# A two-layer transformer block with expert choice and a second mixer block: a reshaped router product, fewer count products, and modulation, squares and weight splits at other places

## Chip, cores and metric

One core of a Trainium2 chip runs the whole program; there is no traffic with other cores. The metric is the device time of one execution in microseconds (us), the median of three runs. The profile is of one execution; its times are microseconds from the start of its span.

## What is computed

512 latent tokens and 256 context tokens of width 1024 go through two layers and then one further block. Cut to what matters:

```python
for l in (0, 1):
    mod  = silu(c)     @ w_ada[l] + b_ada[l]       # 1024 -> 6144: six shifts, scales, gates
    modc = silu(c_ctx) @ w_ada[l] + b_ada[l]       # the same for the context
    h = modulate(rmsnorm(x), sh1, sc1);  p = h @ w_in[l]
    x = x + gt1 * mixer(p)        # two attentions, a short convolution,
                                  # three gated branches, @ w_out
    h2 = modulate(rmsnorm(x), sh2, sc2)
    x = x + gt2 * experts(h2)
# the context takes the same steps in layer 0 only

def experts(h):                                    # 16 experts, hidden 1024
    aff = softmax(h @ w_router, axis=experts)      # w_router: 1024 x 16
    gate, idx = top_k(aff, cap)                    # per expert 64 tokens (context 32)
    y = (silu(h[idx] @ w_g) * (h[idx] @ w_u)) @ w_d
    return scatter_add(y * gate)
```

Layer 1 works on the 512 latent tokens alone. The further block (`x2`) has a norm, a dilated and a latent attention, gated branches, an output product and a two-matrix feed-forward. Everything is float32; large products are made of three rounded-float32 ones.

## The kernel before

**Layout.** Activations stand transposed in on-chip memory: `XT[128, 8, 768]` has channel 128k+p in row k of partition p and the tokens along the columns (512 latent, 256 context). The program is written once for each engine, as functions in stage order (`pe_program`, `act_program`, `dve_program`, `pool_program`, `sp_program`, L2403 to L2497): start, then for each layer projection, attention, merge, choice and experts, then the second block. Nothing reorders the work; each engine takes its instructions in the written order, and counted semaphores tie the engines together.

**Dense products.** `pe_linear3` (L544) computes 128 output channels for all tokens: 8 blocks of 128 channels, three products each (`wh*xh`, `wh*xl`, `wl*xh`), each in a piece of 512 and one of 256 tokens in layer 0. SyncE loads weights in pieces of 512 KB into a ring of six halves (`sp_dense`, L536): piece p waits until piece p-6 is used up. A weight is split in two by ScalarE (`act_high`, L515, writes the rounded high part) and then VectorE (`dve_low`, L526, the rest).

**Modulation.** `w_ada` of both layers is 96 tiles of 128 x 1024 (512 KB), 16 to a pair, three pairs a layer. `pe_mod` (L615) multiplies one tile: four products of 256 columns, each on 32 columns of the array. A pair holds one of the four PSUM banks (`bank`) from its first tile to its last. Then `act_mod` (L633) copies it, `pe_modt` (L639) turns it and `dve_mod` (L648) adds the bias. Pairs 0 to 2 (layer 0) are made in the start and the projection of layer 0, pairs 3 to 5 (layer 1, tiles 48 to 95) in the merge of layer 0.

**Merge** (`pe_merge` L1312, `act_merge` L1338, `dve_merge` L1373). For 24 steps t (three branches of eight): a gate product t; in layer 0 modulation tile 48+2t; at odd t two branch products; tile 49+2t. Pairs are turned at t=8, t=16 and after the first output product. ScalarE's order at t = 7, 15 and 23 in layer 0 is: sigmoid, `act_mod` of the pair (waits for its last tile), then `act_high` of the next weight. Then eight output products; each is added to XT and squared by ScalarE; GpSimd adds up the squares (`pool_square`, L680), and `pe_total` (L698) sums the total over the partitions with a product with ones, once all eight are in. ScalarE makes 1/rms of it in two steps (`act_rstd`).

**Choice** (`pe_choice` L1431, `act_choice` L1499, `dve_choice` L1536). VectorE scales and ScalarE shifts the eight rows to `HT`. The router product takes `HT` in blocks of 128 tokens as the stationary operand and the 16 router columns of a k as the moving one: 8 k times 6 token blocks (4 in layer 1). VectorE makes a softmax, TensorE turns it, VectorE finds the top 64 by eight rounds of maxima (then the context's 32), while TensorE turns `HT` to tokens in rows (`h2`) and ScalarE copies it. Then each expert's chosen tokens are counted by a product of the mask with a triangle (`tri`) and with ones, one product for each pair of token blocks (13 in layer 0, 10 in layer 1), VectorE writes one-hot matrices (`SC` context, `SX` four blocks for the latents), and TensorE gathers the tokens with them, PSUM bank by bank, after the last `SX`.

**Experts** (`pe_experts`, L1856). Expert weights come in loads of 1 MB; the first 5 (layer 0) or 7 (layer 1) fit in beside the stages before (`sp_experts`, L2445; three lie in the ring of the dense weights), the others only after the gather. The last `pe_back` (L1723) adds the outputs of the last experts to XT, one k after another; ScalarE squares each k, and TensorE multiplies the square of k-1 after the product of k. The next stage begins with 1/rms, `act_high` and `dve_low` of its first weight (`act_proj` L916, `dve_proj` L955, `act_second`, `dve_second`), then the normed input. Before the second block SyncE waits for the last k, loads the rope tables, and then the first weights.

## Time and profile before

| | |
|---|---|
| median of 3 runs | 3765.2 us (3760.98 to 3766.6) |
| the profiled execution | 3764.25 us, its span 3762.5 us |
| TensorE (PE) busy in matmuls | 3437.9 us, 91% |
| VectorE (DVE), ScalarE (ACT), GpSimd (POOL) | 33%, 27%, 5% |
| from HBM | 595.55 MB, 159 GB/s over the span |
| TensorE's granted clock, mean | 0.963 of 2.4 GHz |

Stages of the profiled execution: merge of layer 0 about 507 to 932, its choice to 1034, its experts to 1621; choice of layer 1 from 2209, its experts 2290 to 2793; then the second block. How to read it: a busy share is an average over stages with different limits. PE is busy nearly everywhere, so what counts is whether a piece of PE work stands in a stretch that PE fills, or in one where PE waits for another engine; and who is the last to be waited for at each of PE's pauses. A matmul of float32 (not rounded) shows as two records, and matmuls overlap in the records, so the distance of starts says more than the durations.

### The profile page before, as it was taken

The numbers are of one execution on the slowest core, as the hardware profiler recorded it, in microseconds if no ns is written. First come the engines' busy times: TensorE is split into PE (matmuls) and PEld (weight loads), VectorE is DVE, ScalarE is ACT, GpSimd is POOL, SyncE is SP. The second block draws the span as 40 slices with busy tenths as digits, with TensorE's granted clock in tenths as the row PEclk, the third lists the DMA queues.
The fourth block names the chain that finished last, engine by engine and source line by source line (L and its number), as shares of the span: only waits on it lengthen the run. The fifth ranks groups of instructions, "written<-read, shape, count | busy, mean of one in ns | idle before, by whom it ended". The sixth has DMA issues, their size and how long they took to land.

```text
span 3762.5 us, 48664 instructions
## 1 busy us (share of the span) xinstructions
PE 3437.9 (91%) x21614; PEld 2314.7 (62%) x21618; DVE 1250.0 (33%) x1753; ACT 1017.9 (27%) x1619; POOL 190.9 (5%) x124
## 2 busy tenths in 40 slices
PE   7999999998899999989999979888879889979997
PEld 5786677787744344367668864222237756858886
DVE  3226632223421111144653341111133425353333
ACT  3523531212310000055442231000022334242322
POOL 0100000111100000000000120000001010020000
PEclk9999999999799999999999979999999989989999
DMA  6440024341099999812003326999962111313331
GB/s 218 135 129 18 1 74 127 120 130 61 22 368 382 359 347 368 302 40 84 18 12 96 96 84 260 409 409 409 409 231 73 33 35 42 96 52 98 95 98 45
DMA packets 359986, 600.81 MB, mean 160 GB/s; under 512 B 48771, under 2 KB 242657, under 8 KB 359649
## 3 DMA queue, kind: packets, MB, share of 16 engines
q1 hardware_dynamic: 357024, 596.62, 44.9%
q8 instruction: 171, 2.80, 0.3%
q10 hardware_dynamic: 2752, 1.08, 0.1%
q14 instruction: 39, 0.31, 0.0%
HBM read 595.55 MB, written 2.10 MB: 159 GB/s over the span
## 4 chain that ended last, share of the span: by engine, by line
PE 80%; DMA 8%; DVE 5%; SPq 3%; ACT 3%; issue 1%; POOL 0%; ACTq 0%; POOLq 0%; DVEq 0%
PE ps L558 31%; PE ps L1815 6%; PE ps L2160 5%; PE ps L1037 4%; DMA ring<-in_w_e_down 4%; DMA ring<-in_w_e_up 3%; PE ps L606 3%; PE ps L1126 3%; PE ps L1847 3%; PE ps L1818 3%; SPq L2462 3%; PE ps L1087 3%; PE ps L1301 3%; PE ps L577 2%; PE ps L1495 2%; PE ps L1852 1%
## 5 line engine op out<-in xcount | busy, mean ns | idle before, releaser
L558 PE MATMUL ps<-xh,wh 128*128 128x512 f32 x1912 | 650.6, 378 | 49.1 <-DVE xl L2022 18.6
L558 PE MATMUL ps<-xl,wh 128*128 128x512 f32 x1912 | 633.3, 369 | 0.0
L558 PE MATMUL ps<-xh,wl 128*128 128x512 f32 x1912 | 631.7, 368 | 0.0
L533 DVE TENSOR_TENSOR wl<-ring,wh 128x1024 fp32r<-128x1024 f32 (+1 forms) x259 | 333.7, 1289 | 661.9 <-ACT wh L524 660.7
L558 PEld LDWEIGHTS ps<-xh,wh 128*128 128x128 f32 x1912 | 331.4, 190 | 142.2 <-issue 55.7
L524 ACT ACTIVATE wh<-ring 128x1024 fp32r<-128x1024 f32 (+1 forms) x259 | 271.7, 1050 | 466.7 <-PE ps L558 170.7
L558 PEld LDWEIGHTS ps<-xl,wh 128*128 128x128 f32 x1912 | 331.9, 190 | 63.3 <-issue 4.3
L558 PEld LDWEIGHTS ps<-xh,wl 128*128 128x128 f32 x1912 | 331.5, 190 | 62.3
L1815 PE MATMUL ps<-ring,arena 128*32 128x512 f32 x2048 | 267.2, 593 | 1.0 <-DVE arena L1597 1.0
L1810 PE MATMUL ps<-ring,arena 128*64 128x512 f32 x1024 | 235.0, 598 | 30.5 <-DMA ring<-in_w_e_up 16.8
L1810 PEld LDWEIGHTS ps<-ring,arena 128*64 128x64 f32 x1024 | 69.3, 136 | 187.7 <-issue 107.0
L1843 PE MATMUL ps<-ring,hbuf 128*64 128x512 f32 x512 | 125.3, 639 | 42.6 <-DMA ring<-in_w_e_down 41.1
L1818 PEld LDWEIGHTS ps<-ring,arena 128*32 128x32 f32 x2048 | 66.7, 110 | 153.1 <-issue 153.1
L1048 DVE TENSOR_REDUCE sm<-ps 128x2 f32<-128x1536 f32 (+3 forms) x96 | 142.3, 1482 | 46.2 <-PE ps L1037 46.0
L1818 PE MATMUL ps<-ring,arena 128*32 128x256 f32 x2048 | 157.4, 379 | 0.0
L1037 PE MATMUL ps<-arena 64*128 64x256 f32 (+3 forms) x800 | 152.1, 455 | 2.6 <-DVE arena L997 1.8
L1087 PE MATMUL ps<-consts,tmp 128*128 128x128 f32 x832 | 127.0, 284 | 20.3 <-DVE arena L1143 12.0
L1066 ACT ACTIVATE tmp<-ps,sm 128x768 f32<-128x768 f32 (+3 forms) x176 | 132.5, 761 | 46.5 <-DVE sm L1051 39.0
L1964 DVE SCALAR_TENSOR_TENSOR y<-ps,gate,y 128x1024 fp32r<-128x1024 f32 x16 | 20.5, 1284 | 330.5 <-ACT y L1903 330.5
L1087 PEld LDWEIGHTS ps<-consts,tmp 128*128 128x128 f32 x832 | 88.4, 141 | 59.0 <-issue 22.0
L1847 PE MATMUL ps<-ring,hbuf 128*32 128x512 f32 x1024 | 122.9, 598 | 0.8 <-DVE hbuf L1956 0.8
L1843 PEld LDWEIGHTS ps<-ring,hbuf 128*64 128x64 f32 x512 | 42.7, 145 | 120.1 <-issue 118.4
(256 smaller groups left out, 4449.7 us busy)
## 6 DMA issues: line engine op xcount, KB each, us to landing
ring<-in_w_e_gate SPq DMA_DIRECT2D x128, 1024.0 KB, 10.6
ring<-in_w_e_up SPq DMA_DIRECT2D x128, 1024.0 KB, 10.7
ring<-in_w_e_down SPq DMA_DIRECT2D x128, 1024.0 KB, 14.8
ring<-in_w_in SPq DMA_DIRECT2D x116, 512.0 KB, 4.0
ring<-in_w_ada SPq DMA_DIRECT2D x96, 512.0 KB, 4.7
ring<-in_w_ff SPq DMA_DIRECT2D x64, 512.0 KB, 3.9
ring<-in_w_out SPq DMA_DIRECT2D x24, 512.0 KB, 3.8
ring<-in_w_in SPq DMA_DIRECT2D x40, 256.0 KB, 4.1
```

What stands on the lines that cost most here:

```text
L524: e.activation(m.WH[:, o:o + many], halves.aps[s][:, 0:many], ACT.Copy).then_inc(*hi.up(X.key, q))
L533: e.tensor_tensor(m.WL[:, o:o + many], halves.aps[s][:, 0:many], m.WH[:, o:o + many].bitcast(F32), ALU.subtract).then_inc(*lo.up(X.key, q))
L558: i = e.matmul(ps[0:M, a:b], w[:, k, 0:M], h[:, k, a:b], start=k == 0 and p == 0, stop=k == 7 and p == 2)
L1037: x = e.matmul(ps[:, col:col + k.shape[-1]], q, k, start=first, stop=last, skip_group_check=True)
L1048: e.tensor_reduce(mx, A.units(i, A.scores(i)), AX, ALU.max).then_inc(*a_rm.up(A.stage, i))
L1087: x = e.transpose(ps[:, 128 * c:128 * c + 128], src[:, u, 128 * b:128 * b + 128], ident)
L1810: i = e.matmul(pa[64 * h:64 * h + 64, 512 * w:512 * w + 512], XS(kk)[:, x, 0:64], W[:, k, 512 * h:512 * h + 512], start=kk == 0, stop=kk == 7)
L1815: e.matmul(pa[64 * h + g:64 * h + g + 32, 512 * w:512 * w + 512], XS(kk)[:, x, g:g + 32], W[:, k, 512 * h:512 * h + 512], start=kk == 0, s ...
L1818: i = e.matmul(pb[32 * q:32 * q + 32, 256 * w:256 * w + 256], XS(kk)[:, x, 64:96], W[:, k, 256 * q:256 * q + 256], start=kk == 0 and w == ...
L1843: i = e.matmul(ps[64 * x:64 * x + 64, 512 * h:512 * h + 512], HT2[p % 2][:, x, k % 4, k // 4, :], w, start=k == 0, stop=k == 7)
L1847: e.matmul(ps[64 * x + g:64 * x + g + 32, 512 * h:512 * h + 512], HX[:, k, 64 * x + g:64 * x + g + 32], w, start=k == 0, stop=k == 7, skip ...
L2160: i = e.matmul(accs(d), w[:, 0, d * 128:(d + 1) * 128], h[:, f % 8, 0:NX], start=f == 0 and p == 0, stop=f == 31 and p == 2)
```

## The change

Seven edits: (1) modulation pairs 4 and 5 (tiles 64 to 95) leave the merge of layer 0; tiles 64 to 67 stand after the output products, 68 to 79 ahead of the router product, 80 to 87 after it, 88 to 95 after the turning of `HT`; their loads follow those of `w_out` in SyncE's queue; pair 3 stays. (2) The router product has the router columns stationary (32 wide: 16 of k and the 16 beside them) and `HT` moving, k on column group k % 4; ScalarE copies the four partial sums to memory, and a second product folds them with a constant (`fold`) to tokens x experts. (3) The counts are one product with the triangle for all blocks and one with ones for all later blocks. (4) The first four gather products take their four PSUM banks at once and run block by block behind `SX`. In the choice of layer 0 `act_mod(4)` stands after the copy of the partial sums and `act_mod(5)` after the copies of `h2`; `dve_mod(4)` after the softmax, `dve_mod(5)` after the top 32. (5) `pe_total` sums GpSimd's total without the last square, and then the last square itself. (6) The squares in the last `pe_back` stand two k late. (7) The first weight of the next stage is split before the last two squares (ScalarE, at k = 6) and after the last addition (VectorE); before the second block its first six pieces are loaded ahead of the rope tables.

```diff
@@ mixer_weights
+                    if t < 8:
                         mods(48 + 2 * t)
...
+                    if t < 8:
                         mods(49 + 2 * t)
             for d in range(KD):
                 X.split(("o", d), 128, column(I["w_out"][l], 128 * d))
+            mods(*range(64, 96))
@@ sp_dense
+                if p == 6 and between:
+                    between(e)
@@ act_mod, pe_modt
-        MR = tmp[:, 3840:4352]
+        MR = lambda pair: tmp[:, 3840:4352] if pair < 4 else AR(21504, 512)
@@ pe_total
-            e.wait_ge(*l_na.at(stage, kn - 1))
+            e.wait_ge(*l_na.at(stage, kn - 2))
             for a, b in segs(T):
-                i = e.matmul(ps[:, a:b], ones[:, :], total[:, a:b], start=True, stop=True)
+                e.matmul(ps[:, a:b], ones[:, :], total[:, a:b], start=True, stop=False)
+            e.wait_ge(*n_sq.at(stage, kn - 1))
+            for a, b in segs(T):
+                i = e.matmul(ps[:, a:b], ones[:, :], last[:, a:b], start=False, stop=True)
@@ act_proj, dve_proj
+            if l == 0:
                 act_high(e, X, 0)
...
+            if l == 0:
                 dve_low(e, X, 0)
@@ pe_merge (act_merge, dve_merge alike)
-                    if l == 0 and t and t % 8 == 0:
-                        pe_modt(e, 2 + t // 8)
+                    if l == 0 and t == 8:
+                        pe_modt(e, 3)
...
-                    if l == 0:
+                    if l == 0 and t < 8:
                         pe_mod(e, 48 + 2 * t)
...
-                if l == 0 and d == 0:
-                    pe_modt(e, 5)
-            pe_total(e, f"f{l}", KD, T, tmp[:, 2304:3072])
+            if l == 0:
+                for m in range(64, 68):
+                    pe_mod(e, m)
+            pe_total(e, f"f{l}", KD, T, tmp[:, 2304:3072], sqr[0])
@@ pe_choice
+            mods(*range(68, 80))
+            ps, when = bank.take((st, "lgp"), r_act.at(st, "lgp"))
...
             for k in range(KD):
                 e.wait_ge(*r_act.at(st, "h", k))
-                for c in range(ntc):
-                    i = e.matmul(ps[:, 16 * c:16 * c + 16], HT[:, k, c * 128:(c + 1) * 128], wrv[:, l, k, :],
-                                 start=k == 0 and c == 0, stop=k == 7, skip_group_check=True)
+                for a, b in segs(T):
+                    i = e.matmul(ps[32 * (k % 4):32 * (k % 4) + 32, a:b], wr[:, 128 * l + 16 * k:128 * l + 16 * k + 32], HT[:, k, a:b],
+                                 start=k < 4, stop=k > 3, skip_group_check=True)
+            i.then_inc(*p_rt.up(st, "lgp"))
+            mods(*range(80, 88))
...
+            e.wait_ge(*r_act.at(st, "lgp"))
+            for c in range(ntc):
+                i = e.matmul(ps[:, 16 * c:16 * c + 16], L_[1][:, 128 * c:128 * c + 128], K("fold"), start=c == 0, stop=True, skip_group_check=True)
             i.then_inc(*p_rt.up(st, "lg"))
+            if l == 0:
+                pe_modt(e, 4)
...
+            mods(*range(88, 96))
+            if l == 0:
+                pe_modt(e, 5)
...
+            e.matmul(ps[:, 0:16 * ntc], K("tri"), mskT[:, 0:ntc, :], start=True, stop=False, skip_group_check=True)
             for a, b, cap, c0, c1 in sides:
-                for c in range(c0, c1):
-                    for j in range(c0, c + 1):
-                        i = e.matmul(ps[:, 16 * c:16 * c + 16], ones[:, :] if j < c else K("tri"), mskT[:, j, :], start=j == c0, stop=j == c)
+                for j in range(c0, c1 - 1):
+                    i = e.matmul(ps[:, 16 * j + 16:16 * c1], ones[:, :], mskT[:, j:j + 1, :].broadcast_to([128, c1 - 1 - j, 16]), start=False,
+                                 stop=j == c1 - 2, skip_group_check=True)
...
+            for tiles in [[(k, eh) for k in (0, 1) for eh in (0, 1)]] + [[(k, eh)] for k in range(2, KD) for eh in (0, 1)]:
...
+                for c in (1, 2, 3, 0):
+                    e.wait_ge(*r_dve.at(st, "sx", c))
+                    for ps, (k, eh) in zip(taken, tiles):
+                        gather(ps, k, eh, c)
@@ act_choice
+            e.wait_ge(*p_rt.at(st, "lgp"))
+            e.activation(L_[1][:, 0:T], bank.of[st, "lgp"][:, 0:T], ACT.Copy).then_inc(*r_act.up(st, "lgp"))
+            if l == 0:
+                act_mod(e, 4)
...
@@ dve_choice
...
+            if l == 0:
+                dve_mod(e, 4)
...
+            if l == 0:
+                dve_mod(e, 5)
...
@@ pe_back
-                if p == MANY - 1 and k:
-                    pe_square(e, f"n{l + 1}", k - 1, KD, T0 - NC_ * l, norm_bufs(l)[(k - 1) % 2])
-            if p == MANY - 1:
-                pe_square(e, f"n{l + 1}", KD - 1, KD, T0 - NC_ * l, norm_bufs(l)[(KD - 1) % 2])
+                if p == MANY - 1 and k > 1:
+                    pe_square(e, f"n{l + 1}", k - 2, KD, T0 - NC_ * l, norm_bufs(l)[k % 2])
+            for k in (KD - 2, KD - 1) if p == MANY - 1 else ():
+                pe_square(e, f"n{l + 1}", k, KD, T0 - NC_ * l, norm_bufs(l)[k % 2])
@@ act_experts, dve_experts
             for k in range(KD):
+                if k == 6:
+                    act_high(e, WX[l + 1], 0)
...
             dve_back(e, l, MANY - 1)
+            dve_low(e, WX[l + 1], 0)
@@ pool_merge, pool_second
-            for k in range(1, KD):
+            for k in range(1, KD - 1):
@@ sp_program
-            e.wait_ge(*d_xo.at("e1", 7, KD - 1))
-            e.dma_start(AR(Z, 2048), crope[:, 0:2048]).then_inc(s_cr, 16)
-            e.dma_start(ROT, crope[:, 2048:2304]).then_inc(s_cr, 16)
-            sp_dense(e, WX[2], after_experts(1))
+            def ropes(e):
+                e.wait_ge(*d_xo.at("e1", 7, KD - 1))
+                e.dma_start(AR(Z, 2048), crope[:, 0:2048]).then_inc(s_cr, 16)
+                e.dma_start(ROT, crope[:, 2048:2304]).then_inc(s_cr, 16)
...
+            sp_dense(e, WX[2], after_experts(1), ropes)
```

## Rows read from the trace of the kernel before

**Rows 1.** The page: what the DMA engines moved, in 40 equal slices of 94 us.

```profile
GB/s 218 135 129 18 1 74 127 120 130 61 22 368 382 359 347 368 302 40 84 18 12 96 96 84 260 409 409 409 409 231 73 33 35 42 96 52 98 95 98 45
```

**Rows 2.** Windows, merge and router of layer 0: PE, PEld, DVE, ACT, POOL busy, granted clock.

```profile
760.00:800.00 40.00, 40.00 (x254) 32.51 (x254) 11.99 (x9) 7.40 (x8) 7.22 (x4) 1.00 0.43 138
944.00:948.00 4.00, 4.00 (x20) 4.00 (x20) 4.00 (x9) 4.00 (x9) 0.00 (x0) 0.50 0.39 159
```

**Rows 3.** Timeline of PE in the merge: start, us, line, operands, count, idle before.

```profile
514.89 0.53 PE L558 MATMUL ps<-xl,wh 128*128 128x512 f32 x2
...
515.25 0.51 PE L558 MATMUL ps<-xh,wl 128*128 128x512 f32 x2
...
516.70 0.62 PE L558 MATMUL ps<-xh,wh 128*128 128x512 f32 x2
...
524.92 0.52 PE L558 MATMUL ps<-xh,wl 128*128 128x512 f32 x2
...
525.94 0.62 PE L1301 MATMUL ps<-brh,wh 128*128 128x512 f32 x2
```

**Rows 4.** Timelines of PE and of ACT where the third branch begins.

```profile
740.22 1.01 PE L558 MATMUL ps<-xh,wh 128*128 128x512 f32 x2 [2.35 <-DVE tmp L1382]
...
736.50 0.60 ACT L637 ACTIVATE tmp<-ps 128x512 f32<-128x512 f32 x1 [8.88 <-PE ps L627]
```

**Rows 5.** Timelines of PE and of DVE where the output products begin.

```profile
860.35 0.98 PE L558 MATMUL ps<-xh,wh 128*128 128x512 f32 x2 [6.59 <-DVE xl L1401]
...
871.78 0.60 PE L645 MATMUL ps<-consts,tmp 128*128 128x128 f32 x4
...
855.40 1.22 DVE L533 TENSOR_TENSOR wl<-ring,wh 128x1024 fp32r<-128x1024 f32 x1 [17.93 <-ACT wh L524]
```

**Rows 6.** Timeline of the norm and the router product of layer 0.

```profile
935.82 2.90 PE L703 MATMUL ps<-tmp,ones 128*128 128x512 f32 x4 [4.08 <-POOL tmp L684]
...
941.85 8.56 DVE L1545 SCALAR_TENSOR_TENSOR arena<-arena,A,tmp 128x512 f32<-128x512 f32 x16 [8.92 <-ACT tmp L711]
...
943.90 20.63 PE L1441 MATMUL ps<-wr,arena 128*128 128x16 f32 x96 [5.18 <-ACT arena L1505]
```

**Rows 7.** The loads of w_ada (96 of 512 KB), all of them.

```profile
DMA to landing us min/median/max: 3.6/4.7/19.5
```

**Rows 8.** The count products with ones: durations min/median/max, ns.

```profile
L1472 PE MATMUL ps<-aff,ones x26: 374/374/375, 987.6 to 2252.5; 128*128 128x16 f32 x26
```

**Rows 9.** Timelines of POOL, PE, ACT and DVE, norm to gather of layer 1.

```profile
2210.09 1.26 POOL L684 TENSOR_TENSOR tmp<-tmp 128x512 f32<-128x512 f32 x1 [4.15 <-ACT tmp L678]
...
2211.50 2.05 PE L703 MATMUL ps<-tmp,ones 128*128 128x512 f32 x2 [2.94 <-POOL tmp L684]
...
2217.90 13.80 PE L1441 MATMUL ps<-wr,arena 128*128 128x16 f32 x64 [4.35 <-ACT arena L1505]
...
2258.24 0.80 PE L1495 MATMUL ps<-sx,h2h 128*128 128x512 f32 x1 [4.98 <-DVE sx L1591]
...
2217.03 5.36 ACT L1505 ACTIVATE arena<-arena,mod 128x512 f32<-128x512 f32 x8 [0.82 <-DVE arena L1545]
...
2253.55 4.63 DVE L1591 TENSOR_TENSOR sx<-consts,aff 128x1024 fp32r<-128x1024 f32 x4
```

**Rows 10.** Timelines of ACT and DVE after the experts of layer 0.

```profile
1623.27 0.84 ACT L711 ACTIVATE tmp<-tmp 128x768 f32<-128x768 f32 x1
...
1625.10 2.36 DVE L533 TENSOR_TENSOR wl<-ring,wh 128x1024 fp32r<-128x1024 f32 x2 [6.56 <-ACT wh L524]
```

**Rows 11.** Timelines of ACT and DVE after the experts of layer 1.

```profile
2795.02 0.63 ACT L711 ACTIVATE tmp<-tmp 128x512 f32<-128x512 f32 x1
2798.23 1.06 ACT L524 ACTIVATE wh<-ring 128x1024 fp32r<-128x1024 f32 x1 [2.58 <-DMA ring<-in_w_in]
...
2800.46 2.15 DVE L2027 SCALAR_TENSOR_TENSOR tmp<-arena,PT,tmp 128x512 f32<-128x512 f32 x2
```

**Rows 12.** Groups by line: the squares of both last pe_back; busy, mean ns, idle before.

```profile
L695 PE MATMUL ps<-hbuf,ones 128*128 128x512 f32 x32 | 18.3, 656 | 4.4 <-ACT hbuf L678 4.4
```

More of the change, by code:

```diff
@@ L1329, in pe_merge @@
                                      d_wg.at(X.key, t - 1 + dd))
[L1330 removed]
+                    if l == 0 and t < 8:
                         pe_mod(e, 49 + 2 * t)
@@ L1392, in dve_merge @@
                     dve_low(e, X, X.unit["g", br, d] + 1)
-                    if l == 0 and t and t % 8 == 0:
-                        dve_mod(e, 2 + t // 8)
+                    if l == 0 and t == 8:
+                        dve_mod(e, 3)
                     if d % 2:
@@ L1403, in dve_merge @@
                 dve_low(e, X, X.unit["o", d] + 1)
-                if l == 0 and d == 0:
-                    dve_mod(e, 5)
                 e.wait_ge(*dn.at(X.key, X.unit["o", d]))
@@ L1433, in pe_choice, with mods @@
             m = ME[l]
+            def mods(*tiles):
+                for m in tiles if l == 0 else ():
+                    pe_mod(e, m)
+            mods(*range(68, 80))
+            ps, when = bank.take((st, "lgp"), r_act.at(st, "lgp"))
+            for w in when:
+                e.wait_ge(*w)
+            e.wait_ge(s_r, 32)
+            e.wait_ge(*d_st.at("st", "wr0"))
+            for k in range(KD):
+                e.wait_ge(*r_act.at(st, "h", k))
+                for a, b in segs(T):
[3 more added lines that the diff above has]
+            mods(*range(80, 88))
             ps, when = bank.take((st, "lg"), r_dve.at(st, "af"))
@@ L2394, in pool_second @@
                 e.tensor_tensor(MX[:, d, :], MX[:, d, :], work[(8 + d) % 5][:, 0:NX], ALU.add).then_inc(*l_ma.up("x2", 8 + d))
-            for k in range(1, KD):
+            for k in range(1, KD - 1):
                 pool_square(e, "no", k, NX, sqr, tmp[:, 2304:2816])
```

54 lines of the change are left out of this document (26 added, 28 removed).

## The prediction

> **What bounds the kernel now.** I read the windows first, then PE's timeline through the merge and the choice, then the other engines at each of PE's pauses. The merge of layer 0 is PE's: in 40 us it is busy for 40, at full clock, while VectorE and ScalarE have two thirds free [rows 2]. So a product taken out there is won. The choice is a chain instead: norm, router product, softmax, eight rounds of maxima, counts, gather, each waiting for the one before, and PE goes through the router at a granted clock of 0.50, the lower level of 1.2 GHz, though it is busy all the time [rows 2]. The experts of layer 1 are the DMA's: four slices at 409 GB/s [rows 1]. Most of their loads are issued only after the gather, so an earlier gather moves the whole stage.
>
> **Merge of layer 0.** 32 of its 48 tiles go. The groups before and after keep a step of 0.36 us from start to start (514.89 to 515.25). Two tiles in a row stretch one step to 1.45 us, a single one to 1.02 [rows 3]: 1.09 and 0.66 us. From t=8 on there are 8 pairs and 14 singles that PE runs through: 8 x 1.09 + 14 x 0.66 = 17.9 us. The last single of the second and of the third branch are in pauses and are counted with these.
>
> Third branch (t=15 to 16): ScalarE waits 8.88 us for the last tile to copy pair 4 [rows 4], and the split of the next gate weight is queued behind that wait; PE resumes at 740.22. The tile ended at 736.45, so the branch products at 735.8. With pair 4 gone the split is long done: 740.22 - 735.8 = **4.4 us**. (t=7 to 8 keeps its pair.)
>
> Output products: PE stopped at 853.76, less the tile's 0.66 at 853.1, and resumed at 860.35 [rows 5]. VectorE had waited 17.93 us for ScalarE and only then, at 855.40, did a split and two weighings that could have been done. At least 855.40 - 853.1 = 2.3 us goes, at most 7.2; I take 5.0, as the split and the first weighing go too, while the last weighing, copy and subtraction stay. The first output product then took 860.35 to 871.78, 11.4 us, for 24 steps of 0.36 = 8.6: part of the 2.8 over is clock lost in the pause, part the subtractions, which stay; I take 1.8, and 0.6 for the turning [rows 5]. Merge: 17.9 + 4.4 + 5.0 + 2.4 = **29.7 us** (25 to 33).
>
> **Norm and router of layer 0**, where the tiles arrive. PE stopped at 935.82 - 4.08 = 931.74. Tiles 64 to 67, in the ring since the last output weights were split, take 4 x 0.55 = 2.2 us of that pause. The total's product took 2.90 us at half clock [rows 6], so 1.45 at full; now two of them, 2.9, and PE is warm: end 936.8 instead of 938.72, 1.9 earlier. VectorE's and ScalarE's rows (8.56 us, last about 951.2) then end at 949.3.
> Tiles 68 to 79 stand in front of the router. This is the **added wait**: each needs its load, SyncE may issue tile n only when n-6 is used, and behind it on PE wait router, softmax, all. Tile 70 can be issued at 932.3 and lands 4.7 us later [rows 7], the others at 409 GB/s [rows 1] 1.28 us apart: tile 79 at 948.5. It is just covered by the rows of HT.
> The Trainium skill ("DMA: Bandwidth & Descriptors", the table of figures at its head) puts the HBM limit of a core at about 358 GB/s; by it a tile takes 1.46 us, tile 79 comes 1.6 us later and the sum is 1.6 us smaller. The rows with 409 GB/s contradict that limit here.
> The router: 8 k of 768 columns, 1.45 us each at full clock. The nearest row is the modulation tile, whose four column groups run abreast (0.55 us for what would be 4 x 0.48): two rounds, 2.9 us. One after another at half clock it would be 23.2. The two pieces of one k share a group, so I take 7.0: 949.3 to 956.3. Then tiles 80 to 87; 86 and 87 are issued only when 80 and 81 are used, and land 4.7 us later, near 962; the copy of the partial sums (about 0.9) is covered by that. The fold, 12 records between 0.11 and 0.215 us (20.63 us for 96 [rows 6]), ends near 964.6. Now the logits are ready at 943.90 + 20.63 = 964.53. **Sum 0** (5 won with 2.9 and the smallest landing of 3.6; 16 lost with 23.2).
> The last eight tiles and both turnings stand beside 17 us of maxima on VectorE; if that cover were gone they would cost about 8 x 1.28 = 10 us. dve_mod 4 and 5 hide behind transposes. SyncE reaches the first five expert loads some 45 us later than now, when the last tile is used; 5 MB take 13 us at 409 GB/s, and counts and gather of context and latents lie in between (by the stage times 986 to 1034), so nothing is late.
>
> **Counts.** Layer 0 goes from 13 products to 5, layer 1 from 10 to 4; a product is two records, the record 0.215 us apart as in the router [rows 6, 8]: 16 x 0.215 = 3.4 and 12 x 0.215 = 2.6 us. The wider moving operands (up to 96 columns) may hide under the same weight load; if not, they cost 0.5.
> The Trainium skill ("TensorEngine Tiling (Array Packing)", Instruction Overhead) has about 60 cycles of overhead for a matmul; by it a record is some 0.05 us at 1.2 GHz and both edits are worth 1.4 us, not 6.0. The rows say 0.215, four times that.
>
> **Gather.** In layer 1 PE waits 4.98 us for all four SX, 4.63 us of work; three of the four go: 3.5 us [rows 9]. In layer 0 the context's gather covers them; there, taking four banks at once makes PE wait for the last context copy, 0.9 lost (0 to 1.5).
>
> **Norm and router of layer 1.** GpSimd's 1.26 us and the handover go, and PE, fed without its pause of 2.94 us, need not fall to the half clock at which the product takes 2.05 [rows 9]: 1.4 to 2.4, I take 2.0; the same again before the feed-forward of the second block (the third such place, alike). The router now ends at 2217.90 + 13.80 = 2231.7. The changed one is paced by ScalarE's rows, done at 2222.4; then one product of 512 columns, 1.7 to 2.05, a copy of 0.7, 8 records of 0.215: 2226.9. **4.8 us** (3 to 7).
>
> **End of the experts.** PE waits 4.4 us in all for squares in the two last pe_back [rows 12]; two k late, most is filled: 3.5 (0 to 4.4). The early split: in layer 0 1/rms is done at 1624.11 and VectorE is free of the split at 1627.46, 3.35 us [rows 10]; in layer 1, 2795.65 to 2800.46, 4.8 us, the load among it [rows 11]. ScalarE's split waits for its load at k=6, with two squares and 1/rms behind it; the load is issued once the last expert's slot is free, long before. It takes 1.06 us a piece, in a pause of ScalarE in layer 0; in layer 1 it may hold up the last squares by 1. SyncE's rope loads are behind six pieces but keep their own wait, about 5 us ahead of need. Together **11.7 us** (5 to 13).
>
> **Sum:** 29.7 + 0 + 3.4 + 2.6 + 3.5 - 0.9 + 2.0 + 2.0 + 4.8 + 11.7 = 58.8 us. From the profiled execution's 3764.25 that is 3705.5; the median of the runs lies 1 above it, so about **3706**. PE's last stages follow unchanged, and a shift passes through projection, attention and experts whole.
>
> **Rivals.**
> *The router stage of layer 0 pays* (0.20): tiles paced by loads leave PE mostly idle, the clock falls to 1.2 GHz as it does now after 931.74, and the new router runs its groups one by one. For: now 20 us of products leave the clock at 0.50. Cost 8 to 16: 3714 to 3722.
> *The clock stays up* (0.15): steady tiles keep PE at 2.4 GHz, the groups run abreast, counts and context gather (twelve slow products) start fast. 5 at the router, 4 to 6 behind it, up to 3 in the merge: 3692 to 3697.
> *The splits move without shortening* (0.12): loads not there at k=6, or the split on the path of the last squares; or the output pause stays at its lower bound. Loses 7 to 11: 3713 to 3717.
> *Slower* (0.02): the ring gives no overlap, each tile is waited for its whole landing, 4.7 us. Tiles 68 to 87 are then 94 us in front of the fold, which ends near 1034, 69 late, and tiles 88 to 95 (38 us) outlast the 17 us of maxima by 20: 89 - 59 = 30 us slower, 3796. It decides from about 3.7 us a tile on. Against: the ring has six halves, so six loads are in flight.
> *The change does little* (0.01): what leaves the merge comes back whole in the choice. The pauses of rows 4 and 5 speak against it.
> Forecast itself: 0.50.
>
> **How the numbers follow.** The forecast's own range, from the bounds of its terms, is 3697 to 3713. 8 in 10 needs the paying router and the warm clock as well: 3692 to 3722. A measurement of this kernel can tell about 0.2% (7.5 us) from no change. Only the last two rivals are not faster by more: faster 0.97, same 0.01, slower 0.02.
>
> **What would show it.** In the profile after: no pause of PE near the third branch's start, and one of some 2 to 3 us before the output products; PE's tiles ahead of the router with waits on loads of w_ada; the router's groups in 3 to 15 us and a wait for tile 86 before the fold; six records with ones in the counts of layer 1 behind the triangle's two; PE's idle time for squares near 1 us; VectorE's first scaling right behind 1/rms. Wrong it would be if PE stood in the merge elsewhere, if the tiles came slower than 1.5 us apart, or if the clock at the router stayed 0.50 for all of it.

## The result, and the profile after

The changed kernel takes 3700.7 us (median of four runs, 3696.9 to 3702.5) against 3763.7 us beside it on the same chip (3761.0 to 3766.6): a ratio of 0.983, 95% interval 0.981 to 0.985, 63.0 us faster. The forecast was 3706 (3692 to 3722). The profiled execution of the changed kernel is its quickest, 3696.9 us with a span of 3695.1; against the one of before the difference is 67.4 us. So a sum made from the rows of the two traces has to give 67, and 4 of it are this one execution.

The page of the changed kernel, what the DMA engines moved in its 40 slices (compare with [rows 1]):

```profile
GB/s 222 131 131 24 1 59 119 63 58 140 188 374 353 385 345 359 267 52 86 7 20 95 92 86 330 409 409 409 409 212 74 35 39 35 92 59 97 96 97 46
```

The plateau of 409 in the experts of layer 1 has the same height and length as before; the loads are not faster, they begin earlier. To see where the time went, take the start of one and the same event in both traces and subtract. A link is the stretch between one event and the next; the fourth column is what it gained, the last what was forecast for it.

| event | before | after | link gained | forecast |
|---|---|---|---|---|
| first tile in the merge | 515.70 | 514.03 | 1.7 | ahead of every edit |
| end of the output products | 931.74 | 896.88 | 33.2 | 29.7 |
| end of the product(s) with ones | 938.72 | 901.58 | 2.3 | 1.9 |
| logits read by VectorE | 964.57 | 929.47 | -2.0 | -1.9 (the stage: 0) |
| first one-hot matrix (`SC`) | 993.25 | 953.91 | 4.2 | 3.4 |
| first expert product, layer 0 | 1035.39 | 996.87 | -0.8 | -0.9 |
| first scaling, layer 1 | 1627.37 | 1582.88 | 6.0 | 11.7 for both ends of experts |
| end of output products, layer 1 | 2208.60 | 2167.12 | -3.0 | 0 |
| first scaling to `HT` | 2216.24 | 2172.51 | 2.2 | 2.0 |
| logits read, layer 1 | 2231.74 | 2181.61 | 6.4 | 4.8 |
| first `SX` | 2253.55 | 2200.24 | 3.2 | 2.6 |
| first expert product, layer 1 | 2291.23 | 2234.35 | 3.6 | 3.5 |
| first scaling, second block | 2800.46 | 2734.83 | 8.7 | (in the 11.7) |
| product with ones, second block | 3341.66 | 3273.64 | 2.4 | 2.0 |

**The merge.** PE's timeline of the changed kernel where the third branch begins and where the output products begin; they answer to [rows 4, 5]:

```profile
723.62 0.51 PE L1314 MATMUL ps<-brh,wl 128*128 128x512 f32 x2
723.96 0.51 PE L564 MATMUL ps<-xh,wh 128*128 128x512 f32 x2
724.31 0.51 PE L564 MATMUL ps<-xl,wh 128*128 128x512 f32 x2
...
824.68 0.51 PE L1314 MATMUL ps<-brh,wl 128*128 128x512 f32 x2
827.27 0.59 PE L564 MATMUL ps<-xh,wh 128*128 128x512 f32 x2 [2.08 <-DVE xl L1415]
...
829.69 1.01 PE L564 MATMUL ps<-xh,wh 128*128 128x512 f32 x2 [1.12 <-DVE xl L1415]
```

The first has no pause at all, 0.35 us from start to start. The second has kept 2.08 and 1.12 us of waits for VectorE's subtraction.

**Norm and router of layer 0**, the same view, with [rows 6] as its counterpart:

```profile
898.74 1.56 PE L710 MATMUL ps<-tmp,ones 128*128 128x512 f32 x4
900.13 1.45 PE L713 MATMUL ps<-tmp,ones 128*128 128x512 f32 x4
901.52 1.93 PE L633 MATMUL ps<-ring,cs 128*32 128x256 f32 x32
904.24 0.64 PE L633 MATMUL ps<-ring,cs 128*32 128x256 f32 x8 [0.79 <-DMA ring<-in_w_ada]
905.52 0.64 PE L633 MATMUL ps<-ring,cs 128*32 128x256 f32 x8 [0.64 <-DMA ring<-in_w_ada]
907.79 0.97 PE L633 MATMUL ps<-ring,cs 128*32 128x256 f32 x8 [1.63 <-DMA ring<-in_w_ada]
909.51 1.08 PE L633 MATMUL ps<-ring,cs 128*32 128x256 f32 x8 [0.76 <-DMA ring<-in_w_ada]
...
913.29 1.08 PE L633 MATMUL ps<-ring,cs 128*32 128x256 f32 x8 [0.19 <-DMA ring<-in_w_ada]
914.57 1.08 PE L633 MATMUL ps<-ring,cs 128*32 128x256 f32 x8 [0.20 <-DMA ring<-in_w_ada]
915.43 4.14 PE L1459 MATMUL ps<-arena,wr 128*32 128x512 f32 x32
919.39 2.46 PE L633 MATMUL ps<-ring,cs 128*32 128x256 f32 x40
...
924.34 0.64 PE L633 MATMUL ps<-ring,cs 128*32 128x256 f32 x8 [1.25 <-DMA ring<-in_w_ada]
925.67 1.08 PE L633 MATMUL ps<-ring,cs 128*32 128x256 f32 x8 [0.69 <-DMA ring<-in_w_ada]
926.68 2.74 PE L1468 MATMUL ps<-consts,arena 128*128 128x16 f32 x12
```

Read it by the brackets. Tiles 72 to 79 wait for loads of `w_ada` and come 1.24 to 1.28 us apart, but for two steps: tile 74 is 2.27 behind 73 and tile 75 1.72 behind 74. The load of tile 74 waits until tile 68 is used, and tile 68 stands behind the products with ones (901.52); SyncE issues it at 902.22. The router is 4.14 us; then tiles 85 to 87 wait for loads again (two of the three are shown), and the fold stands behind them. ScalarE's rows and its copy of the partial sums, from its timeline:

```profile
905.50 8.53 ACT L1544 ACTIVATE arena<-arena,mod 128x512 f32<-128x512 f32 x16 [0.82 <-DVE arena L1589]
919.69 0.81 ACT L1547 ACTIVATE arena<-ps 128x768 f32<-128x768 f32 x1 [5.66 <-PE ps L1459]
```

The rows were there at 914.03, so the router began 1.4 us late, which is what the two long steps add up to, and ended 5.5 us behind the last row (919.57). The copy was there at 920.50, so tiles 80 to 87 held the fold back by 6.2. The windows of the stretch (PE, PEld, DVE, ACT, POOL busy, granted clock, DMA share, GB/s):

```profile
900.00:904.00 4.00, 3.45 (x38) 1.61 (x36) 0.00 (x0) 2.65 (x4) 0.00 (x0) 1.00 1.02 400
909.00:917.00 8.00, 6.75 (x48) 1.60 (x52) 4.28 (x9) 5.03 (x10) 0.00 (x0) 0.50 1.01 400
914.00:918.00 4.00, 3.80 (x30) 1.20 (x27) 0.00 (x0) 0.03 (x1) 0.00 (x0) 0.50 1.03 417
```

In these windows the DMA share is 1.01 to 1.03 at 400 to 417 GB/s, and PE, with waits between its tiles, sinks from 2.4 to 1.2 GHz (granted 1.00, then 0.50). It is back at 1.00 from 919 to 925 and at 0.50 again when the fold comes.

**Layer 1 and the ends of the experts.** PE in the norm and router (compare [rows 9]), the squares by line ([rows 12]), and VectorE's split and first scaling in layer 0 and before the second block ([rows 10, 11]):

```profile
2166.91 1.02 PE L710 MATMUL ps<-tmp,ones 128*128 128x512 f32 x2
2168.59 1.13 PE L713 MATMUL ps<-tmp,ones 128*128 128x512 f32 x2 [0.65 <-ACT tmp L684]
2174.16 5.59 PE L1459 MATMUL ps<-arena,wr 128*32 128x512 f32 x16 [4.45 <-ACT arena L1544]
2180.53 1.04 PE L1468 MATMUL ps<-consts,arena 128*128 128x16 f32 x8 [0.78 <-ACT arena L1547]
```

```profile
1576.98 2.35 DVE L537 TENSOR_TENSOR wl<-ring,wh 128x1024 fp32r<-128x1024 f32 x2
1582.88 2.21 DVE L841 SCALAR_TENSOR_TENSOR tmp<-arena,A,tmp 128x512 f32<-128x512 f32 x4 [3.55 <-ACT tmp L721]
...
2729.11 1.22 DVE L537 TENSOR_TENSOR wl<-ring,wh 128x1024 fp32r<-128x1024 f32 x1
2734.83 2.17 DVE L2078 SCALAR_TENSOR_TENSOR tmp<-arena,PT,tmp 128x512 f32<-128x512 f32 x2 [4.50 <-ACT tmp L721]
```

```profile
L701 PE MATMUL ps<-hbuf,ones 128*128 128x512 f32 x32 | 16.5, 601 | 1.7 <-ACT hbuf L684 1.7
```

In both places VectorE's split now ends before ScalarE has 1/rms (1579.33 against 1582.84 in layer 0), and what the first scaling waits for is 1/rms alone.

### The profile page after: what moved, and what is told of

It reads as the page before. It is cut to its first block, busy times and chain, and to the rows that moved or that the text cites. A ratio compares the mean times of both kernels' runs of the same rounds, so it can differ in the third digit from the quotient of the medians.

```text
span 3695.1 us, 48440 instructions
## 1 busy us (share of the span) xinstructions
PE 3406.1 (92%) x21502; PEld 2284.0 (62%) x21506; DVE 1248.2 (34%) x1754; ACT 1019.5 (28%) x1621; POOL 186.5 (5%) x121
## 4 chain that ended last, share of the span: by engine, by line
PE 80%; DMA 8%; DVE 5%; SPq 3%; ACT 3%; issue 1%; ACTq 0%; POOL 0%; POOLq 0%; DVEq 0%
PE ps L564 32%; PE ps L1863 6%; PE ps L2211 5%; DMA ring<-in_w_e_down 4%; PE ps L1050 4%; DMA ring<-in_w_e_up 4%; PE ps L612 3%; PE ps L1139 3%; PE ps L1866 3%; PE ps L1895 3%; SPq L2511 3%; PE ps L1100 3%; PE ps L1314 3%; PE ps L583 2%; PE ps L1520 2%; PE ps L1900 1%
## 5 line engine op out<-in xcount | busy, mean ns | idle before, releaser
L564 PE MATMUL ps<-xh,wh 128*128 128x512 f32 x1912 | 651.9, 379 | 35.8 <-DVE xl L2073 11.4
## 6 DMA issues: line engine op xcount, KB each, us to landing
ring<-in_w_e_gate SPq DMA_DIRECT2D x128, 1024.0 KB, 10.4
ring<-in_w_e_up SPq DMA_DIRECT2D x128, 1024.0 KB, 10.4
```

The costliest lines, as they stand in the source:

```text
L564: i = e.matmul(ps[0:M, a:b], w[:, k, 0:M], h[:, k, a:b], start=k == 0 and p == 0, stop=k == 7 and p == 2)
```

## The experiments

Seven kernels undo one edit each in the changed kernel; two put one thing into the kernel before; one measures the column groups; two go further. "+" is against 3700.7. The kernel before was measured beside each and came out at 3763.7 to 3766.5 us. Taken against it, the "+" of six of the undone edits is 2.6 to 2.8 us smaller than given below (merge, router, counts, sum of squares, squares, split; the gather's is 0.2 smaller), and the 95% interval of each ratio is about 5 us wide to either side. So a difference of 4 to 9 us is not clear by the medians alone; what carries these readings are the links. In the traces of these kernels I subtract links, as in the table; the changed kernel's own trace, its quickest run, is 0.6 to 1.2 us shorter than nearly all others in some links that an edit doesn't touch, which is taken off below.

**The merge edit undone.** All 32 tiles back in the merge, everything else as changed.

```diff
-                    if l == 0 and t < 8:
+                    if l == 0:
                         pe_mod(e, 48 + 2 * t)
...
-            mods(*range(68, 80))
...
-            mods(*range(80, 88))
...
-            mods(*range(88, 96))
```

> The changed kernel with tiles 64 to 95 back in the merge of layer 0, all else as changed. Theory: the merge is 33 us longer again (17.9 for the tiles in the running stream, the two pauses, the first output product), but the choice of layer 0 gets back what its tiles cost there: rows of HT end at about 914, router and copy one after the other with no tile between, so the logits come about 10 us earlier relative to the norm. Net +23, near 3724 us. Rival, as predicted (the tiles in the choice are free): the full +33, near 3734. Rival (tiles cost the same wherever they stand): 3701.

3720.2 us, +19.5. In its trace first tile to end of output products is 32.3 us longer, and from the product with ones to the logits it is 10.4 shorter: router from 941.57 to 950.36, paced by the rows of HT, and the fold 1 us behind it. So the tiles cost the choice 10, the first theory; "free" falls. 6.2 of it is the fold's wait. The other 4 are ahead of the router: without tiles it runs along with the rows and ends 1.5 us behind the last (948.84), with them 5.5 behind.

**The merge edit alone**, in the kernel before (the same diff the other way round, old router, old counts and the rest).

> The kernel before with the first edit alone: tiles 64 to 95 leave the merge, 64 to 67 behind the output products, 68 to 79 ahead of the old router product, 80 to 87 right behind it, 88 to 95 behind HT's turning. Theory (a tile costs the choice only where it keeps the logits back, which here only 68 to 79 do, by 1 to 2 us): merge -32, choice +1.5, near 3734 us, so the edit is worth 30 here although undoing it in the changed kernel costs only about 20 to 23. Rival (the choice pays 10 us for the tiles wherever they stand in it): near 3743.

3747.2 us against 3765.5, 18.3 faster, not 31: a miss. Products with ones begin 33.0 us earlier in the link, as expected. But logits come 7.4 us later behind them, and `SC` another 6.8:

```profile
920.43 1.08 PE L633 MATMUL ps<-ring,cs 128*32 128x256 f32 x8 [0.19 <-DMA ring<-in_w_ada]
921.44 20.66 PE L1453 MATMUL ps<-wr,arena 128*128 128x16 f32 x96
942.04 5.35 PE L633 MATMUL ps<-ring,cs 128*32 128x256 f32 x48
...
950.50 0.82 PE L1464 MATMUL ps<-consts,aff 128*16 128x128 f32 x6
```

I had compared the end of the tiles with the last row of HT. The old router is PE's own 20.6 us and starts with the first row, 8.1 us after the product with ones [rows 6]; behind the tiles it starts 15.4 after it. And tiles 80 to 87, right behind the router, keep the softmax's result waiting for its turning (950.50) for 8.35 us after the logits. So the same tiles cost 7.4 us ahead of a product that is PE's own time and 4 ahead of one that the rows pace.

**The router undone.** HT stationary again, no copy and fold, tiles 80 to 87 behind it.

```diff
-                for a, b in segs(T):
-                    i = e.matmul(ps[32 * (k % 4):32 * (k % 4) + 32, a:b], wr[:, 128 * l + 16 * k:128 * l + 16 * k + 32], HT[:, k, a:b],
...
+                for c in range(ntc):
+                    i = e.matmul(ps[:, 16 * c:16 * c + 16], HT[:, k, c * 128:(c + 1) * 128], wrv[:, l, k, :],
```

> The changed kernel with the router product as before (HT stationary, 96 and 64 records, no copy and no fold); tiles 80 to 87 stand right behind it. Theory (records 0.215 us apart at the lower clock): layer 0 from 915.4 plus 20.6 gives logits at 936 instead of 929.3, +6.7; layer 1 +6.4; together +13, near 3714 us. Rival (steady tiles keep the clock up, so records are 0.11 apart): layer 0 ends at 926, so 3 us better than changed, layer 1 +6: near 3704.

3723.1 us, +22.4, more than either theory. To the logits it is +5.6 in layer 0 (6.8 in the trace, less 1.2; 96 records in 20.66 us from 919.37 on, 0.215 apart) and +6.0 in layer 1, as the first theory has it; another 6.4 are again tiles 80 to 87, which here stand ahead of the softmax's turning and keep `SC` back. That part belongs to where this kernel puts them, not to the router. These links make 18, against 22.4, or 19.7 when it is taken against the kernel before beside it (3766.5).

**One column group.** All eight k on the first 32 columns.

```diff
-                    i = e.matmul(ps[32 * (k % 4):32 * (k % 4) + 32, a:b], wr[:, 128 * l + 16 * k:128 * l + 16 * k + 32], HT[:, k, a:b],
-                                 start=k < 4, stop=k > 3, skip_group_check=True)
+                    i = e.matmul(ps[0:32, a:b], wr[:, 128 * l + 16 * k:128 * l + 16 * k + 32], HT[:, k, a:b],
+                                 start=k == 0, stop=k == KD - 1, skip_group_check=True)
```

> The changed kernel with all eight k of the router product on the first 32 columns of the array, one sum instead of four partial ones, and the fold over 32 rows. Theory (four column groups run abreast): in layer 0 the eight products then follow each other at 1.39 us each, which is what two products of 768 columns with ones stand apart in the changed kernel, 11.1 us instead of 4.0 from start to end: +7 in layer 0 (up to +16 if at the lower clock); in layer 1 ScalarE's rows set the pace, +0 to 1. Near 3708 us. Rival (the groups do not overlap, the saving came from fewer records alone): no change in either layer, 3701.

3709.4 us, +8.7.

```profile
920.63 11.29 PE L1459 MATMUL ps<-arena,wr 128*32 128x512 f32 x31
931.75 0.38 PE L1459 MATMUL ps<-arena,wr 128*32 128x256 f32 x1
```

11.5 us instead of 4.1: the groups do run abreast. The clock wasn't the same in both: it was 0.50 for the first 2 us of the 11.5 and 1.00 from 924 on, and 0.50, then 0.70 for the first 4 of the 4.1. So the one group had the faster clock, and at one clock the gap would be wider. The logits are only 4 late, since the tiles' loads arrive meanwhile. In layer 1 it is +3.6, which I had put at 0 to 1: the granted clock is 0.50 from 2184 to 2188, and 14 records take 7.94 us, 1.13 a k, where ScalarE's row takes 0.67. The Trainium skill ("TensorEngine Tiling (Array Packing)", When to Use Tiling) advises this swap with four column tiles where the moving side has 32 columns, and its table under Theoretical Speedup gives up to 4 times; 11.5 over 4.1 is 2.8 here.

**The counts undone**, 13 and 10 products.

```diff
-            e.matmul(ps[:, 0:16 * ntc], K("tri"), mskT[:, 0:ntc, :], start=True, stop=False, skip_group_check=True)
...
+                for c in range(c0, c1):
+                    for j in range(c0, c + 1):
+                        i = e.matmul(ps[:, 16 * c:16 * c + 16], ones[:, :] if j < c else K("tri"), mskT[:, j, :], start=j == c0, stop=j == c)
```

> The changed kernel with 13 and 10 count products instead of 5 and 4. Theory (a record of a small product costs 0.215 us at the lower clock): +3.4 and +2.6, near 3706.5 us. Rival (an overhead of about 60 cycles a record, 0.05 us): +1.4, near 3702. In the profile the counts of layer 0 take 5.7 us instead of 1.8 from first to last.

3707.3 us, +6.6. By link it is 4.2 less 0.8 in layer 0 and 3.2 less 0.6 in layer 1 (what other kernels with the edit in place have more than the changed one's trace): 3.4 and 2.6, the prediction's two numbers. The wide operand costs nothing that shows. The Trainium skill's 60 cycles a product (the same page, Instruction Overhead) would have made it 1.4; the links of these runs contradict that for float32 products of 128 stationary columns.

**The gather undone**, bank by bank behind all four `SX` (`e.wait_ge(*r_dve.at(st, "sx", 0))` ahead of it).

> The changed kernel with the gather bank by bank, after all four SX. Theory: layer 1 waits for three more one-hot blocks, +3.5; layer 0 gets back the 0.85 that taking four banks at once cost; near 3703.5 us. Rival (the first four banks only wait elsewhere, for the copies of the fifth): no change, 3701.

3705.2 us, +4.5. From the first `SX` to the second block 3.6 us longer; layer 0 gives back up to 1.2. As expected; by the median alone the rival (3701) would not be excluded.

**The sum of squares undone**: GpSimd adds all eight, one product.

```diff
-            e.wait_ge(*l_na.at(stage, kn - 2))
+            e.wait_ge(*l_na.at(stage, kn - 1))
...
-                i = e.matmul(ps[:, a:b], ones[:, :], last[:, a:b], start=False, stop=True)
```

> The changed kernel with GpSimd adding the last square too and one product with ones per total. Theory (GpSimd's addition and its handover leave the chain, and PE stays at full clock): +2.2 in layer 1, +2.2 in the second block, +1 to 2 in layer 0, where four tiles and the loads of the next ones cover part of it; near 3706.5 us. Rival (the gain in layer 1 and the second block was the clock alone, the product taking 2.05 instead of 1.0): the wait for GpSimd shows under 1 us and the sum is +2, 3703.

3707.4 us, +6.6; by link 0.7 in layer 0, 1.7 in layer 1, 2.5 in the second block. PE's row in layer 1 of this kernel shows the wait for GpSimd that the changed one lacks, and the half clock with it, so the rival of "the clock alone" falls:

```profile
2174.85 2.04 PE L710 MATMUL ps<-tmp,ones 128*128 128x512 f32 x2 [2.94 <-POOL tmp L690]
```

**Squares one k late again.**

```diff
-                if p == MANY - 1 and k > 1:
-                    pe_square(e, f"n{l + 1}", k - 2, KD, T0 - NC_ * l, norm_bufs(l)[k % 2])
...
+                if p == MANY - 1 and k:
+                    pe_square(e, f"n{l + 1}", k - 1, KD, T0 - NC_ * l, norm_bufs(l)[(k - 1) % 2])
```

> The changed kernel with the squares in the last back products one k late again. Theory: PE waits for ScalarE's square behind most k again, +4.1 in layer 1, +1.2 in layer 0, near 3706 us; the wait in front of the squares grows from 1.7 to about 4.4 us. Rival (the wait only moves to the next link, VectorE's additions): no change, 3701.

3708.0 us, +7.3: 1.8 in layer 0, 4.4 in layer 1. The group's row has its wait of before back:

```profile
L701 PE MATMUL ps<-hbuf,ones 128*128 128x512 f32 x32 | 18.4, 657 | 4.8 <-ACT hbuf L684 4.8
```

3.1 us of waits more than in the changed kernel, but 6.2 of time. With one k between, back product, VectorE's addition, ScalarE's square and the square's product are one round trip: in layer 1 two k take 3.56 us (2732.19 to 2735.75), where in the changed kernel one takes 1.32 (2722.97 to 2724.28). The clock falls besides: 0.71 from 2728 to 2732, where the changed kernel has 1.00 from 2718 to 2734.

**The early split undone**, with the rope tables first again.

```diff
-                if k == 6:
-                    act_high(e, WX[l + 1], 0)
...
-            dve_low(e, WX[l + 1], 0)
```

> The changed kernel with the first weight of the next stage split at the head of that stage again, and the rope tables loaded ahead of the second block's weights. Theory: VectorE's first scaling stands behind its split, +3.4 in layer 0 and +4.8 ahead of the second block, near 3709 us. Rival (the split at k = 6 holds up the last squares, so part of the gain is paid for): +5, 3706, and the squares end earlier without it.

3709.2 us, +8.5: 3.2 in layer 0, 3.6 before the second block. The links make 6.8, between the two theories (8.1 and 5). In the changed kernel VectorE's addition of k = 6 in layer 0 ends at 1574.38 and ScalarE's square of it begins at 1574.59, so the split before it costs at most 0.2.

**Only the pauses**, in the kernel before: ScalarE splits the next weight before it waits for the pair's last tile. No tile moves.

```diff
-                    if l == 0 and t % 8 == 7:
-                        act_mod(e, 3 + t // 8)
                     if d % 2:
                         act_high(e, X, X.unit["b", br, d] + 1)
+                    if l == 0 and t % 8 == 7:
+                        act_mod(e, 3 + t // 8)
```

> The kernel before with one thing changed: at t = 7, 15 and 23 ScalarE splits the next weight before it waits for the pair's last tile. No tile moves. Theory (pauses are the split queued behind the copy): 2.3 us at t = 8 and again at t = 16 (copy and turning stay in the way), 3.3 at the output products, together 8, near 3756 us. Rival (the pauses are the tile, the copy and the turning themselves): no change, 3764.

3752.8 us against 3766.5, 13.7 faster, where I had 8: 4.0 from the turning of pair 3 to that of pair 4, 4.1 from there to the last tile, 5.7 to the product with ones. The first two pauses were 2.35 us each by the row (at the second, 3.8 us lie between the last tile's end and the gate product, with only the turning, 0.63 us, in them); the windows from the start of the third branch say what the rest is. The first two rows are the kernel before, the last two this one:

```profile
740.00:742.00 2.00, 1.78 (x5) 1.59 (x6) 2.00 (x3) 1.92 (x3) 1.76 (x1) 0.51 0.76 205
742.00:744.00 2.00, 2.00 (x9) 1.68 (x8) 2.00 (x2) 0.00 (x0) 2.00 (x2) 0.63 1.10 313
```

```profile
737.00:740.00 3.00, 3.00 (x19) 2.61 (x18) 3.00 (x4) 1.82 (x3) 0.00 (x0) 1.00 0.14 41
740.00:742.00 2.00, 2.00 (x13) 1.74 (x12) 1.41 (x4) 0.00 (x0) 0.00 (x0) 1.00 0.00 0
```

After this pause PE works at the lower level for some 3 us: 14 records in four microseconds where two then hold 13. This pause cost itself and about 1.7 us more. Moving all 32 tiles in the kernel before gained 18.3 us, this swap in ScalarE's order 13.7, so most of what the merge edit is worth there can be had without moving a tile. The swap beside the other six edits, with the tiles left in the merge, was not run.

**Tiles 80 to 87 behind the fold.**

```diff
-            mods(*range(80, 88))
...
                 pe_modt(e, 4)
+            mods(*range(80, 84))
...
                 i.then_inc(*p_rt.up(st, "h2", c))
-            mods(*range(88, 96))
+                mods(84 + 2 * c, 85 + 2 * c)
```

> The changed kernel with tiles 80 to 87 moved: 80 to 83 behind the fold, 84 to 95 two by two behind the six blocks of HT's turning. Theory (these tiles wait for loads and keep the fold back while its operand has long been copied): the fold starts at about 920.7 instead of 926.7, and the maxima of 17 us cover all 16 tiles: 6 us faster, near 3695 us. Rival (the loads are what counts, so the wait goes to the turning of HT and then to the mask): no change, 3701, and VectorE or PE shows a new wait for the last tile's turning or for the copies of h2.

3695.8 us, 4.9 faster than the changed kernel (ratio to before 0.981, 0.980 to 0.983). In the trace the logits come 8.0 us less behind the router's start, 6.8 of them the fold's wait and 1.3 its clock, and no new wait shows up before `SC` (that link differs by 0.4), so the rival falls; the 4.9 of the medians is within their error. The fold waits for the copy alone now, and runs at full clock:

```profile
919.27 3.44 PE L1459 MATMUL ps<-arena,wr 128*32 128x512 f32 x32
923.74 1.48 PE L1467 MATMUL ps<-consts,arena 128*128 128x16 f32 x12 [1.04 <-ACT arena L1547]
...
925.64 1.93 PE L633 MATMUL ps<-ring,cs 128*32 128x256 f32 x32
927.50 0.82 PE L1477 MATMUL ps<-consts,aff 128*16 128x128 f32 x6
```

**All of it together.** With that, the third pair's copy behind the split and its turning behind the next gate product; tiles 64 to 66 ahead of the output products; the router in two halves with tiles between.

```diff
                     pe_linear3(e, X, ("g", br, d), 128, T, (X.key, "g", t), g_sg.at(X.key, t))
+                    if l == 0 and t == 8:
+                        pe_modt(e, 3)
...
             for d in range(KD):
+                if l == 0 and d == 0:
+                    for m in range(64, 67):
+                        pe_mod(e, m)
...
-            mods(*range(68, 80))
+            mods(*range(70, 76))
...
             for k in range(KD):
+                if k == 4:
+                    mods(*range(76, 80))
```

> The same, and with it: at t = 7 ScalarE splits the next weight ahead of the copy of pair 3, which is turned only behind the next gate product (a pause of 4.4 us, 0.6 of it kept, and 1.7 of lower clock behind it: 5); tiles 64 to 66 in the pause ahead of the output products (about 2 with the clock); the router product in two halves of four k with tiles between, tiles 70 to 75 ahead, 76 to 79 between, 80 and 81 behind (3 to 4, since the first four rows of HT are there early). Theory: 16 us faster than the changed kernel, near 3684 us. Rival (what is won ahead of the norm comes back as waits for the loads, as the ring gives 1.28 us a tile whatever stands between): only the 5 of the third pair and the fold's 6, 3690.

3683.9 us (3680.3 to 3686.4), 16.9 faster than the changed kernel, ratio to before 0.9785 (0.977 to 0.980). This is the fastest of all that ran.

```profile
823.18 1.50 PE L635 MATMUL ps<-ring,cs 128*32 128x256 f32 x24
825.33 0.58 PE L566 MATMUL ps<-xh,wh 128*128 128x512 f32 x2 [0.65 <-DVE xl L1420]
...
910.45 1.68 PE L1466 MATMUL ps<-arena,wr 128*32 128x512 f32 x9
...
913.97 1.48 PE L1475 MATMUL ps<-consts,arena 128*128 128x16 f32 x12
```

The wait before the output products is 0.65 instead of 2.08, the products behind the second wait start 0.35 to 0.45 apart at granted 1.00 (0.64 to 0.80 at 0.50 in the changed kernel), and the logits come 11.4 us less after the product with ones than in the changed kernel.

## Why the prediction was right, and where it was not

**The range and the side** were right, and so was the likeliest case: 5 us above the median. Of the rivals, the clock that stays up gave 3692 to 3697; the median is between it and the forecast. Its 3 us in the merge came, its gains at the router and behind it did not: the granted clock was 0.50 from 909 to 917 and from 927 to 931. That was the condition of the first rival, the router stage that pays; but the column groups ran abreast (4.14 us), which it had denied. The signs named for the forecast were there: no pause at the third branch, 2.08 us before the output products, waits for `w_ada` ahead of the router and ahead of the fold.

Against the traces the sum is short by more than against the medians: 58.8 forecast, 67.4 measured, of which 4.4 are the luck of the two executions profiled (3.8 of it the changed kernel's). The terms below say where the rest lies.

**Merge, 29.7, measured 33.2 (32.3 by the undone edit).** The stream of tiles was right. What was too small is the step "PE resumes at 740.22. [...] 740.22 - 735.8 = 4.4 us" and its sister before the output products: from the first gate product of t = 8 to that of t = 16 it was 117.3 us and is 102.7; of these 14.6, 9.0 are tiles and 5.6 the pause. From there to the first output product it was 120.1 and is 103.3; 16.8 less 9.0 is 7.8, not 5.0. I priced a pause at its length and left out the slow products behind it. I had counted that only for the first output product, 2.4 with the turning, and there it did not come: that product went from 11.8 to 11.3 us, as its waits of 2.08 and 1.12 us stayed and a stretch at 0.50 came behind the second. The rest of the 1.8 that the trace has behind this point is the seven other output products, 8.32 us each instead of 8.48; other kernels with the same products (`fold_first`, `u_gather`) have 8.48 too, so that is the execution and not the edit.

**Norm and router of layer 0, sum 0, measured +0.3.** Right in its steps, and right in sum partly by luck: tile 79 was forecast just covered by the rows and was 1.4 late, the router forecast at 7.0 was 4.1, and the wait for the loads of tiles 86 and 87 came, with the fold at half clock behind it. The 1.4 is a step left out: the loads from tile 74 on wait for tile 68, which the products with ones hold back. And the sum of 0 hid 10 us that the tiles cost and as much that the router and the products with ones won. The prediction asked whether the tiles end before the last row, and let the router start there; without tiles the new router is all but done by then. Putting the fold first and halving the router took most of the 10 back. And "one after another at half clock it would be 23.2" was too high a bound: on one group it took 11.5, as the clock rose to 1.00 on the way.

**Counts 3.4 and 2.6, gather 3.5 and -0.9, products with ones 2.0 each**: measured 3.4, 2.6, 3.6, about -1, 2.2 and 2.4. The counts are those of the undone edit; the table's links have 0.8 and 0.6 more. For the counts the distance of records, read from the trace of before, was all that was needed.

**Router of layer 1, 4.8, measured 6.4** (6.0 by the undone edit): I let the last product take 1.7 to 2.05 and the fold's records 0.215. PE was back at full clock when the fold came, its 8 records 1.04 us in all.

**End of the experts, 11.7, measured 14.7.** The squares were the mis-sized term: 3.5, measured 6.2 by undoing them, because they were priced by the wait that the group's row shows. The early split was 8.15, measured 6.8. The two make 13.0; the other 1.7 of the 14.7 no experiment places.

**A term that was missing: -1.5.** The first weight after the wait in layer 1's projection ran at full clock before and at half after, at the same wait of 2.56 us (windows of the kernel before and, in the second fence, after):

```profile
1652.00:1654.00 2.00, 1.58 (x9) 1.45 (x10) 0.88 (x2) 1.36 (x2) 0.00 (x0) 1.00 0.18 43
```

```profile
1608.00:1610.00 2.00, 1.74 (x5) 1.58 (x6) 0.88 (x2) 1.20 (x2) 0.00 (x0) 0.50 0.30 70
```

That is half of the 3.0 that the table loses between the first scaling and the output products of layer 1. Of the rest about 1 is this execution; what remains is not settled. "A shift passes through projection, attention and experts whole" was thus too simple by a microsecond or two.

**The DMA.** The Trainium skill ("DMA: Bandwidth & Descriptors", the table of figures at its head) has about 358 GB/s for a core from HBM; under Measured the same page gives that figure for two cores of a domain streaming at once, and here one core runs. So the prediction set its rows against a figure for another load. Where tiles waited for their loads one after another they came 1.24 to 1.28 us apart, and windows show 400 to 422 GB/s. The rows, by which the forecast went, were right.

The seven single undoings add up to 75 us against 3700.7, and to 59 when each is taken against the kernel before beside it; the change is worth 63. So the medians don't show whether the edits overlap. By trace one part does: 6.4 of the router's undoing are tiles 80 to 87 at a place of that kernel's own.

## What to carry to other kernels

Work that waits for its own loads may be put into a pause only behind everything that the pause's chain needs from that engine: ask of each piece what stands behind it in the same queue, not only whether the engine is idle there. Before moving work out of a full stretch, look at what an engine holds back by waiting in its written order: swapping two instructions of ScalarE at three steps gained 13.7 us where moving 32 tiles gained 18.3. A pause of TensorE can be worth more than its length, as the products behind it may run at half clock; and a row "idle before" can miss half of what a round trip between engines costs (3.1 us by the row, 6.2 by the undone edit). A product with few moving columns is priced by its records, so turn it round or widen it.

## Unexpected of the hardware

- A pause of 2.35 us by the row in a stream at full clock was followed by some 3 us at 0.50 to 0.63, about 1.7 us lost; but one and the same wait of 2.56 us cost nothing in one kernel and 1.5 us in another.
- With tiles and router products in turn, the best kernel's records interleave: products of k on one column group and tiles on others run at the same time (router records from 904.18 to 912.98, the products of tiles 76 to 81 among them from 907.28 on; the first tile's record starts at 907.28 and a router record at 907.29, and six of the 16 router records of the first four k start after it, though they are written ahead of it).
- 32 router records on four column groups took 3.4 to 4.1 us, on one group 11.5.
- PE is busy for all 20.6 us of the old router and the granted clock stays at 0.50 (944 to 964 in the kernel before). The new router begins at 0.50 too, and the clock is at 0.70 from 917 to 919 and at 1.00 from 919 on.
